# Sparse attention issued head by head, with the depthwise taps of the first channels divided between TensorE and VectorE

## The chip, the cores and the metric

One core of a Trainium2 chip runs the whole program. The metric is the device time of one execution in microseconds. Five engines take part: PE (TensorE matmuls, with its weight loads as a row of their own, PEld), DVE (VectorE), ACT (ScalarE), POOL (GpSimd) and SP (SyncE, which only issues DMAs here). Each engine runs its own instruction list in order and waits on semaphores that the others raise.

## The reference, cut to what matters

One decoder layer over 1024 tokens of width 1024, float32. One projection feeds three mixers; their outputs go through an output projection and a layer norm, then through a mixture of experts and a second layer norm. The change touches the mixers' second half, from the end of the search for the top-k bound to the start of the output projection:

```python
# A: sparse attention, 8 heads, blocks of 128 queries (b = 0..7), causal, top 256 keys of an index score
idx_score = jnp.where(causal, einsum('bqhs,bqh->bqs', relu(logits), iw), -inf)
_, sel = lax.top_k(idx_score, topk)
s = einsum('bqhr,bqkr->bqhk', q_b, c_kv[sel]);  p = softmax(s);  o_lat = einsum('bqhk,bqkr->bqhr', p, c_kv[sel])
# B: pooling over 2/4/8/16 positions, a 64x64 map per group, a scale
# C: GLU, depthwise causal convolution of width 31 over 256 channels, layer norm over channels, silu
h = conv(a * sigmoid(gate), conv_w) + conv_b;  y_c = silu(layer_norm(h, ln_g, ln_b))
mix = concat([y_a, y_b, y_c]) @ w_o
```

The kernel doesn't gather keys: it computes all causal scores of a block (128 queries by `WIDTH[b]` = 128(b+1) keys) and adds a bias that is 0 for chosen keys and very negative for the others.

## The kernel before, in words

All names are those of the source; L numbers are its lines.

**Search.** For blocks 7 to 2 the bound that separates the top 256 scores is found by 25 rounds of bisection (`ROUNDS`). In each round DVE counts over blocks 7, 6 and 2 (L1254) and ACT over blocks 5, 4 and 3 (L955), and DVE updates the bounds (L1269 to L1272). Between its counts ACT copies out projection results; from round to round it takes two of the 16 small `key` and `val` matmul units (PE L605 and L609, ACT L913 and L916), which go through four PSUM banks.

**Convolution.** The 256 channels lie in two halves of 128 partitions. The second half's 31 taps are all on POOL: a multiply (L1613) and an add (L1615) of 128x1024 per tap. Of the first half's taps PE does 18 (`TAPS_PE`) as matmuls with diagonal matrices (L660, two 128x512 matmuls a tap) once all units are through; ACT copies the sum out (L969, which raises `conv0`). POOL does the other 13 after its own 31, again with a multiply and an add each (L1646, L1648).

**Attention.** `attention_steps` writes one list of steps, `STEPS`, and each engine walks through it and does its part of each step. A *pair* is two heads (2j, 2j+1) of one block; there are 32 pairs, the first 16 of blocks 0 to 3 (`SHORT_PAIRS`), then four pairs each of blocks 4, 5, 6 and 7. For a pair:

- `qk`: PE computes the scores of one head and then of the other (L687). A head's 64 channels are partitions 0 to 63 or 64 to 127 of `qT` and `keyT`, so the matmuls use 64 rows of the array. DVE adds the bias, negates, and takes the row extremum in one custom instruction (L1329, "the mask" below). ACT takes the exponential with the row sum (L986).
- `pt`: PE transposes the probabilities (L696), two key blocks of both heads into one PSUM bank of a ring; ACT copies the bank into `pT` (L994).
- `pv`: PE multiplies with the values (L711), and after a pair's last group ACT copies 128x128 into `mix` (L998).
- `choose`: DVE turns the bound of a block into its bias row, in seven instructions (L1286 to L1298). They are strewn among the scores, four a pair at first, then one a pair, then two.
- `rl_set`, `rl`: at a block's end DVE makes the reciprocals of the row sums (L1339, L1340), PE transposes them (L719), DVE multiplies them in (L1345).

The ring has three banks. The scores of the next pair are issued one or two pairs ahead, two heads back to back. After block 6 come `cm` (PE L737, the channel mean, which waits for all taps), `csq`, `cv` (the variance, 128x512 matmuls, ACT takes the root L1011), then `cr` (four DVE reciprocals of 128x256, L1354) and `cn` (DVE multiplies L1359, ACT silu L1015).

**Output projection.** When all steps are done ACT and DVE split `mix` and `w_o` into high and low parts (L1027, L1366, L1369), eight rows of `MIX_ORDER`, and PE multiplies them (L415 to L417).

## Time and profile before

| | |
|---|---|
| median of 3 runs | 1118.24 us (1117.61 to 1118.54) |
| the profiled execution's own time | 1117.91 us |
| its span | 1116.1 us |
| PE busy | 944.8 us (85%) |
| DVE busy | 690.5 us (62%) |
| ACT busy | 564.8 us (51%) |
| POOL busy | 398.5 us (36%) |

The span runs from the first to the last instruction in the trace; the rest of the execution's own time lies around it. Times of events below are counted from the span's start. The stretch that the change touches lies between 194 and 474 us; the output projection, the routing and the experts follow it and are as they were.

### The profile page before, as it was taken

The numbers are of one execution on the slowest core, as the hardware profiler recorded it, in microseconds if no ns is written. First come the engines' busy times: TensorE is split into PE (matmuls) and PEld (weight loads), VectorE is DVE, ScalarE is ACT, GpSimd is POOL, SyncE is SP. The second block draws the span as 40 slices with busy tenths as digits, with TensorE's granted clock in tenths as the row PEclk, the third lists the DMA queues.
The fourth block names the chain that finished last, engine by engine and source line by source line (L and its number), as shares of the span: only waits on it lengthen the run. The fifth ranks groups of instructions, "written<-read, shape, count | busy, mean of one in ns | idle before, by whom it ended". The sixth has DMA issues, their size and how long they took to land.

```text
span 1116.1 us, 15675 instructions
## 1 busy us (share of the span) xinstructions
PE 944.8 (85%) x4724; PEld 729.0 (65%) x4725; DVE 690.5 (62%) x990; ACT 564.8 (51%) x796; POOL 398.5 (36%) x241
## 2 busy tenths in 40 slices
PE   6999999687876778699992599999999999999920
PEld 5877888133443444488882478888887888888820
DVE  4259888985656664463757366688888854334316
ACT  4266576963644446650121265678777744324323
POOL 0000299999999980000000111222323221211116
PEclk8999999888978989999995599999999999999975
DMA  8441120000000000162433747999999988554254
GB/s 230 116 114 38 27 87 1 0 1 0 1 1 1 1 1 1 39 189 85 189 141 121 294 168 233 339 386 397 395 394 399 392 293 264 175 132 106 44 150 189
DMA packets 60972, 171.14 MB, mean 153 GB/s; under 512 B 17120, under 2 KB 31456, under 8 KB 48608
## 3 DMA queue, kind: packets, MB, share of 16 engines
q1 hardware_dynamic: 53584, 143.85, 34.7%
q0 software_dynamic: 7056, 25.69, 9.5%
q10 hardware_dynamic: 288, 1.05, 0.3%
q8 instruction: 24, 0.39, 0.1%
q14 instruction: 20, 0.16, 0.0%
HBM read 141.73 MB, written 26.21 MB: 150 GB/s over the span
## 4 chain that ended last, share of the span: by engine, by line
PE 44%; DMA 12%; DVE 7%; issue 4%; ACT 4%; POOLq 0%; POOL 0%; ACTq 0%; DVEq 0%; SPq 0%
PE ps L415 11%; PE ps L417 10%; PE ps L416 10%; DMA raw<-in_w_gate 10%; PE ps L687 3%; PE ps L696 2%; PE ps L711 2%; ACT probs L986 2%; DVE wlo L1521 2%; PE ps L814 1%; PE ps L763 1%; ACT whi L1070 1%; DVE sm L1389 1%; DMA xg<-x_d,idx_now 1%; PE ps L757 1%
## 5 line engine op out<-in xcount | busy, mean ns | idle before, releaser
L1521 DVE TENSOR_TENSOR wlo<-raw,whi 128x2048 fp32r<-128x2048 f32 x96 | 216.0, 2287 | 52.3 <-ACT whi L1070 51.4
L1070 ACT CAST whi<-raw 128x2048 fp32r<-128x2048 f32 x96 | 180.5, 1911 | 72.6 <-DMA raw<-in_w_gate 41.9
L415 PE MATMUL ps<-whi,xgT_hi 128*128 128x512 f32 x384 | 153.0, 398 | 6.9 <-DVE xgT_lo L1531 6.9
L417 PE MATMUL ps<-whi,xgT_lo 128*128 128x512 f32 x384 | 150.8, 393 | 0.0
L416 PE MATMUL ps<-wlo,xgT_hi 128*128 128x512 f32 x384 | 150.5, 392 | 0.0
L1329 DVE CUSTOM_DVE_ANT_0 probs<-ps,bias 128x128 f32<-128x128 f32 (+7 forms) x64 | 46.0, 755 | 83.1 <-PE ps L687 67.4
L415 PE MATMUL ps<-xT_hi,w_hi 128*128 128x512 f32 (+1 forms) x224 | 87.8, 392 | 4.8 <-DVE w_lo L1159 3.1
L1613 POOL TENSOR_SCALAR tapped<-hpad,par 128x1024 f32<-128x1024 f32 x30 | 89.5, 2984 | 2.9
L415 PEld LDWEIGHTS ps<-whi,xgT_hi 128*128 128x128 f32 x384 | 73.0, 190 | 23.0 <-issue 5.8
L1677 POOL COPY idx_now<-slot_token 128x1 int32 (+1 forms) x24 | 7.5, 313 | 223.2 <-PE ps L814 223.2
L416 PE MATMUL ps<-xT_lo,w_hi 128*128 128x512 f32 (+1 forms) x224 | 86.8, 388 | 0.0
L417 PE MATMUL ps<-xT_hi,w_lo 128*128 128x512 f32 (+1 forms) x224 | 86.6, 387 | 0.0
L696 PE MATMUL ps<-ident,probs 128*128 128x128 f32 x288 | 52.8, 306 | 38.9 <-ACT probs L986 28.6
L417 PEld LDWEIGHTS ps<-whi,xgT_lo 128*128 128x128 f32 x384 | 72.7, 189 | 15.5
L416 PEld LDWEIGHTS ps<-wlo,xgT_hi 128*128 128x128 f32 x384 | 72.8, 190 | 14.4
L1692 POOL DMA_INDIRECT acc_d<-ysb,idx_add x24 | 42.3, 1764 | 105.3 <-ACT ysb L1097 105.3
L986 ACT ACTIVATE probs<-probs,sm 128x128 f32<-128x128 f32 (+7 forms) x64 | 49.1, 768 | 60.5 <-DVE sm L1329 60.5
L415 PE MATMUL ps<-whi,hT_hi 128*128 128x512 f32 x192 | 76.9, 401 | 2.7 <-DVE hT_lo L1543 2.7
L1254 DVE TENSOR_SCALAR_CACHE_REDUCE junk_dve<-bias,sm 128x1024 bf16<-128x1024 f32 (+2 forms) x75 | 75.7, 1009 | 1.8
L417 PE MATMUL ps<-whi,hT_lo 128*128 128x512 f32 x192 | 75.1, 391 | 0.0
L416 PE MATMUL ps<-wlo,hT_hi 128*128 128x512 f32 x192 | 74.9, 390 | 0.0
L696 PEld LDWEIGHTS ps<-ident,probs 128*128 128x128 f32 x288 | 33.4, 151 | 62.6 <-issue 60.3
(273 smaller groups left out, 1934.2 us busy)
## 6 DMA issues: line engine op xcount, KB each, us to landing
raw<-in_w_gate SPq DMA_DIRECT2D x32, 1024.0 KB, 12.5
raw<-in_w_up SPq DMA_DIRECT2D x32, 1024.0 KB, 12.4
raw<-in_w_down SPq DMA_DIRECT2D x32, 1024.0 KB, 10.7
w_raw<-in_w_in SPq DMA_DIRECT2D x14, 512.0 KB, 4.0
x_tok<-in_x SPq DMA_DIRECT2D x8, 512.0 KB, 7.5
wo_raw<-in_w_o SPq DMA_DIRECT2D x16, 256.0 KB, 2.7
x_res<-in_x SPq DMA_DIRECT2D x16, 256.0 KB, 3.4
x_d<-xa SPq DMA_DIRECT2D x4, 512.0 KB, 6.5
```

Source lines behind the costliest of these rows:

```text
L415: pe.matmul(out, l_hi, r_hi, start=start, stop=False)
L416: pe.matmul(out, l_hi, r_lo, start=False, stop=False)
L417: return pe.matmul(out, l_lo, r_hi, start=False, stop=stop)
L687: last = pe.matmul(scores_at(u, WIDTH[b])[:, c:c + n], qT[rows, h // 2, b * P:(b + 1) * P], keyT[rows, h // 2, c:c + n], start=True, stop= ...
L696: last = pe.transpose(out[:, c:c + P], probs_at(score_no(b, 2 * j + h))[:, k * P:(k + 1) * P], ident[:])
L986: act.activation(row, row, ACT.Exp, bias=negmax[:, c:c + 1], scale=-1.0, accum_out=rowsum[:, c:c + 1]).then_inc(exped, 1)
L1070: act.copy(whi[:, n, :], raw[:, n, :]).then_inc(gu_hi if n < 4 else dn_hi, 1)
L1254: dve.tensor_scalar(junk_dve[:, 0:WIDTH[b]], bias[:, AT[b]:AT[b] + WIDTH[b]], now[:, c:c + 1], 0.0, ALU.is_lt, ALU.add, accum_out=res[:, c ...
L1329: dve.tensor_tensor_reduce(out=probs_at(u)[:, 0:WIDTH[b]], in0=scores_at(u, WIDTH[b]), in1=bias[:, AT[b]:AT[b] + WIDTH[b]], scale=-1.0, sc ...
L1521: dve.tensor_tensor(wlo[:, n, :], raw[:, n, :], f32(whi[:, n, :]), ALU.subtract).then_inc(gu_lo if n < 4 else dn_lo, 1)
L1613: pool.tensor_scalar(tapped[:], src, by, None, ALU.mult).then_inc(conv1_mul, 1)
L1692: pool.indirect_dma_start(acc_d, bass.IndirectOffsetOnAxis(ap=idx_add[:], axis=0), ysb[:], None, compute_op=ALU.add).then_inc(y_out, 16)
```

## The change

It rewrites `attention_steps` and what hangs on it:

- The unit is one head (`SCORES`), not a pair. Scores are issued three heads ahead (`AHEAD`), one head at a time. The exponential is a step of its own, two heads ahead. A `pt` group now holds key blocks of one head: all of them for blocks 0 to 3, half of them (`groups`) for blocks 4 to 7. The transposes of a group come ahead of the product of the group before it.
- The ring has two banks instead of three; the freed bank gives the product two banks in turn, so that a pair's product waits for the copy of the pair before the last.
- A `choose` instruction follows every head's scores (two in the first four), not every pair's.
- The 18 taps of PE come earlier: the `key` and `val` units use banks 0, 1, 2 and 7, and from the fifth unit on PE does one tap ahead of each unit, and the last six behind them. The scores of the first three heads are issued before the search has ended.
- The 13 taps of POOL on the first channels go to DVE, fused (multiply and add in one instruction), one behind each of the heads 46 to 58 of 64. POOL does nothing for the first channels.
- `cm` stands three heads before the end, `cv` is 16 matmuls of one column with a root and a reciprocal of 128x8, and two `cb` units spread the result over the channels. The silu moves into the output projection, whose order is now 4, 5, 0, 1, 2, 3, 6, 7.

```diff
-MIX_ORDER = [4, 5, 6, 7, 0, 1, 2, 3]
+MIX_ORDER = [4, 5, 0, 1, 2, 3, 6, 7]
...
+TAPS_DVE = range(46, 46 + TAPS - TAPS_PE)
+TAPS_EARLY = 18
...
+def groups(b):
+
+    cut = (b + 2) // 2 if b >= 4 else b + 1
+    return [range(0, cut)] + ([range(cut, b + 1)] if b >= 4 else [])
+
+
+SCORES = [(b, h) for b, j in PAIRS for h in (2 * j, 2 * j + 1)]
+AHEAD = 3
...
+    for u in range(AHEAD):
+        scores(u)
+    for u in range(2):
+        steps.append(("exp", *SCORES[u]))
+    steps.append(("conv0",))
...
+    for u, (b, h) in enumerate(SCORES):
+        if u + AHEAD < len(SCORES):
+            scores(u + AHEAD)
+        for n in range(len(groups(b))):
+            by_dve = False
+            unit("pt", b, h, n, act=not by_dve, dve=by_dve)
+            if n == 0 and u + 2 < len(SCORES):
+                steps.append(("exp", *SCORES[u + 2]))
+            if waiting:
+                product()
+            waiting.append((b, h, n))
+        while ended:
+            unit("rl", ended.pop(0), act=False, dve=True)
...
+        if u in TAPS_DVE:
+            steps.append(("tap", u - TAPS_DVE[0]))
...
+        def unit_bank(k):
+            return ps[:, 4 + k % 4 if k < PROJECTIONS else (0, 1, 2, 7)[k % 4], :]
...
+            taps = 0
+            for k, between in PLAN[1:]:
+                if k >= PROJECTIONS + 4:
+                    tap(taps)
+                    taps += 1
+                unit(k, between)
+            for w in range(taps, TAPS_EARLY):
+                tap(w)
...
-                    out = ps[:, 4 + r % 3, :]
+                    out = ps[:, 4 + r % 2, :]
...
+                elif kind == "tap":
+                    _, n = step
+                    w = TAPS_PE + n
+                    if n == 0:
+                        dve.wait_ge(conv0, 1)
+                    else:
+                        dve.wait_ge(conv0_rest, n)
+                    dve.scalar_tensor_tensor(conv[:, 0, :], hpad[:, 0, w:w + S], convw[:, w:w + 1], conv[:, 0, :],
+                                             ALU.mult, ALU.add).then_inc(conv0_rest, 1)
...
-            for n, w in enumerate(range(TAPS_PE, TAPS)):
-                pool.tensor_scalar(tapped[:], hpad[:, 0, w:w + S], convw[:, w:w + 1], None, ALU.mult).then_inc(conv0_mul, 1)
-                pool.wait_ge(conv0_mul, n + 1)
-                pool.tensor_tensor(conv[:, 0, :], conv[:, 0, :], tapped[:], ALU.add).then_inc(conv0_rest, 1)
-                pool.wait_ge(conv0_rest, n + 1)
```

How the change moves instructions shows best in three places. A row is one instruction, or `x3` like ones, with what it waits for. First PE in the middle of block 7, before: the scores of two heads stand together, then come groups of four transposes and four products.

```order
L687 MATMUL ps<-keyT,qT 128x512 [waits masked_max]
L687 MATMUL ps<-keyT,qT 128x512
L687 MATMUL ps<-keyT,qT 128x512 [waits masked_max]
L687 MATMUL ps<-keyT,qT 128x512
L696 MATMUL ps<-ident,probs 128x128 [waits exped,ring_dve,ring_act]
L696 MATMUL ps<-ident,probs 128x128 x3
L711 MATMUL ps<-pT,value 64x128 [waits ring_act,mixed]
L711 MATMUL ps<-pT,value 64x128 x3
L696 MATMUL ps<-ident,probs 128x128 [waits exped,ring_dve,ring_act]
L696 MATMUL ps<-ident,probs 128x128 x3
```

The same engine in the same block in the changed kernel (scores L700, transposes L710, products L723):

```order
L700 MATMUL ps<-keyT,qT 128x512 [waits masked_max]
L700 MATMUL ps<-keyT,qT 128x512
L710 MATMUL ps<-ident,probs 128x128 [waits exped,ring_dve,ring_act]
L710 MATMUL ps<-ident,probs 128x128 x3
L723 MATMUL ps<-pT,value 64x128 [waits ring_act]
L723 MATMUL ps<-pT,value 64x128 x3
L710 MATMUL ps<-ident,probs 128x128 [waits exped,ring_dve,ring_act]
L710 MATMUL ps<-ident,probs 128x128 x3
L723 MATMUL ps<-pT,value 64x128 [waits ring_act]
L723 MATMUL ps<-pT,value 64x128 x3
L700 MATMUL ps<-keyT,qT 128x512 [waits masked_max]
```

The scores of a head now stand alone between products and transposes, twice as many times. The second place is PE during the search, where before the units come in one run and the taps behind them:

```order
L605 MATMUL ps<-cT,wuk 128x512 [waits wuk_in,unit_dve,unit_act]
L605 MATMUL ps<-cT,wuk 128x512 [waits unit_dve,unit_act] x7
L609 MATMUL ps<-wuv,cT 128x512 [waits wuv_in,unit_dve,unit_act] x8
L660 MATMUL ps<-hpad,diag 128x512 [waits pads_set,idx_relu,diag_set,unit_dve,unit_act]
L660 MATMUL ps<-hpad,diag 128x512
```

and in the changed kernel (units L610 and L614, taps L661):

```order
L610 MATMUL ps<-cT,wuk 128x512 [waits wuk_in,idx_relu,unit_dve,unit_act]
L610 MATMUL ps<-cT,wuk 128x512 [waits unit_dve,unit_act] x3
L661 MATMUL ps<-hpad,diag 128x512 [waits pads_set,diag_set,unit_dve,unit_act]
L661 MATMUL ps<-hpad,diag 128x512
L610 MATMUL ps<-cT,wuk 128x512 [waits unit_dve,unit_act]
L661 MATMUL ps<-hpad,diag 128x512 [waits diag_set]
L661 MATMUL ps<-hpad,diag 128x512
```

Two tap matmuls now stand ahead of each of the last twelve units. The third place is DVE among the heads of blocks 0 to 3. Before, one `choose` instruction (L1292, L1294) follows two masks (L1329, each with a short row that reads its accumulator):

```order
L1292 SCALAR_TENSOR_TENSOR tie_no<-tied 128x384
L1329 ISA probs,sm<-ps,bias 128x128 [waits ring_mm,qk_mm,dve_chain]
L1329 ISA sm 128x1
L1329 ISA probs,sm<-ps,bias 128x128 [waits ring_mm,qk_mm]
L1329 ISA sm 128x1
L1294 SCALAR_TENSOR_TENSOR tied<-tie_no,sm,tied 128x384
```

and in the changed kernel one follows each mask (L1352):

```order
L1352 ISA probs,sm<-ps,bias 128x128 [waits qk_mm,dve_chain]
L1352 ISA sm 128x1
L1317 SCALAR_TENSOR_TENSOR tied<-tie_no,sm,tied 128x384
L1352 ISA probs,sm<-ps,bias 128x512 [waits ring_mm,qk_mm,dve_chain]
L1352 ISA sm 128x1
L1319 SCALAR_TENSOR_TENSOR tied<-tied,above 128x384
L1352 ISA probs,sm<-ps,bias 128x512 [waits ring_mm,qk_mm,dve_chain]
```

Of the 42 `choose` instructions, 22 stood in the first half of the heads (blocks 0 to 3); now 36 do.

## Rows read from the trace of the kernel before

**Rows 1.** Windows: stretch, length; busy (count) of PE, PEld, DVE, ACT, POOL; TensorE clock

```profile
269.00:326.00 57.00, 43.74 (x305) 24.57 (x303) 37.13 (x91) 32.49 (x99) 55.18 (x21) 0.89 0.00 1
326.00:389.00 63.00, 44.66 (x320) 27.58 (x320) 38.92 (x51) 27.19 (x61) 60.92 (x23) 0.86 0.00 1
425.00:469.00 44.00, 36.48 (x270) 21.68 (x268) 22.38 (x31) 29.15 (x49) 0.00 (x0) 0.97 0.08 25
```

**Rows 2.** Waits from 260 to 471 us: total us, times, longest

```profile
DVE probs L1329 <- PE ps L687: 67.4, 15, 13.4
ACT probs L986 <- DVE sm L1329: 60.5, 29, 3.1
```

**Rows 3.** Timeline: units and taps on PE, end of the search, first mask

```profile
194.62 3.59 PE L605 MATMUL ps<-cT,wuk 128*128 128x512 f32 x8
...
226.22 1.05 ACT L916 COPY value<-ps 128x512 f32<-128x512 f32 x2
...
247.10 0.17 DVE L1277 TENSOR_TENSOR sm<-sm 128x6 f32<-128x6 f32 x1
...
249.69 10.47 PE L660 MATMUL ps<-hpad,diag 128*128 128x512 f32 x24
...
260.71 0.29 DVE L1329 CUSTOM_DVE_ANT_0 probs<-ps,bias 128x128 f32<-128x128 f32 x1 [13.45 <-PE ps L687]
```

**Rows 4.** Timeline: block 3's scores of two heads; first transposes of block 4

```profile
283.56 1.13 PE L687 MATMUL ps<-keyT,qT 64*128 64x512 f32 x4
284.61 0.44 PE L696 MATMUL ps<-ident,probs 128*128 128x128 f32 x2
...
326.72 1.09 PE L696 MATMUL ps<-ident,probs 128*128 128x128 f32 x4 [2.78 <-ACT probs L986]
```

**Rows 5.** Chain of work in block 7, in order of time: start, length

```profile
443.29 0.63 PE ps L696 x4
443.92 0.59 PE ps L711 x8
...
445.68 1.93 PE ps L687 x8
...
451.43 0.63 PE ps L696 x4
```

**Rows 6.** Groups of one line on DVE, 247 to 471 us: busy, mean ns, idle before

```profile
L1329 DVE CUSTOM_DVE_ANT_0 probs<-ps,bias 128x128 f32<-128x128 f32 (+7 forms) x64 | 46.0, 755 | 83.1 <-PE ps L687 67.4 <-issue 15.4
L1292 DVE TENSOR_TENSOR_SCAN tie_no<-tied 128x512 f32<-128x512 f32 (+5 forms) x6 | 12.9, 2154 | 0.1
L1296 DVE SCALAR_TENSOR_TENSOR tied<-tied,above 128x512 f32<-128x512 f32 (+5 forms) x6 | 12.3, 2044 | 0.1
L1298 DVE TENSOR_SCALAR bias<-tied 128x512 f32<-128x512 f32 (+5 forms) x6 | 10.5, 1749 | 0.1
L1290 DVE SCALAR_TENSOR_TENSOR tied<-bias,sm,above 128x512 f32<-128x512 f32 (+5 forms) x6 | 9.1, 1525 | 0.1
L1294 DVE SCALAR_TENSOR_TENSOR tied<-tie_no,sm,tied 128x512 f32<-128x512 f32 (+5 forms) x6 | 9.0, 1504 | 0.1
...
L1286 DVE TENSOR_SCALAR_CACHE_REDUCE above<-bias,sm 128x512 f32<-128x512 f32 (+5 forms) x6 | 5.7, 943 | 0.1
L1345 DVE TENSOR_TENSOR mix<-mix,ps 128x512 f32<-128x512 f32 x8 | 5.5, 686 | 11.3 <-PE ps L719 11.1
```

**Rows 7.** Groups by shape, all engines, 260 to 471 us: busy, mean ns, idle before

```profile
L994 ACT COPY pT<-ps 128x512 f32<-128x512 f32 x64 | 36.4, 578 | 28.3 <-PE ps L696 28.2
...
L986 ACT ACTIVATE probs<-probs,sm 128x1024 f32<-128x1024 f32 x8 | 9.2, 1148 | 10.1 <-DVE sm L1329 10.1
...
L1290 DVE SCALAR_TENSOR_TENSOR tied<-bias,sm,above 128x1024 f32<-128x1024 f32 x1 | 1.3, 1285 | 0.0
```

**Rows 8.** Chain of work at the end of attention: start, length

```profile
469.41 0.70 PE ps L719 x4
...
474.24 0.77 PE ps L415
```

More of the change, by code:

```diff
@@ L87, in score_no, with last_score @@
     return 2 * PAIR_NO[b, h // 2] + h % 2
[L90 to L92 removed]
+def groups(b):
[3 more added lines that the diff above has]
+AHEAD = 3
+def last_score(b):
+    return max(u for u, x in enumerate(SCORES) if x[0] == b)
 def attention_steps():
[L100 removed]
     steps, ring, r_of = [], [], {}
@@ L108, in unit, with scores, product @@
         ring.append((act, dve))
-    def rowsums(p):
-        b = pairs[p][0]
-        if p >= 0 and p == last_no(b):
-            steps.append(("rl_set", b))
-    def scores(p):
-        b, j = pairs[p]
+    def scores(u):
+        b, h = SCORES[u]
         while choices and any(x[1] == b for x in choices):
             steps.append(choices.pop(0))
-        for h in range(2):
-            steps.append(("qk", b, 2 * j + h))
-        rowsums(p - 1)
-        for _ in range(min(4 if p < 2 else 1 if p < SHORT_PAIRS else 2, len(choices))):
+        steps.append(("qk", b, h))
+        for _ in range(min(2 if u < 4 else 1, len(choices))):
             steps.append(choices.pop(0))
-    def after_block(b):
-        unit("rl", b, act=False, dve=True)
-    scores(0)
-    scores(1)
+    def product():
+        b, h, n = waiting.pop(0)
+        steps.append(("pv", b, h, n))
+        if score_no(b, h) == last_score(b) and n == len(groups(b)) - 1:
+            ended.append(b)
+    for u in range(AHEAD):
[3 more added lines that the diff above has]
+    steps.append(("conv0",))
     for i in range(2):
@@ L134, in attention_steps @@
             unit("pw", i, c, act=True, dve=False)
-    ahead = 2
-    waiting = []
-    def product():
-        b, j, n = waiting.pop(0)
-        steps.append(("pv", b, j, n))
-        return b if n == b // 2 and j == HEADS // 2 - 1 else None
-    for p, (b, j) in enumerate(pairs):
-        ended = None
-        for n in range(b // 2 + 1):
-            unit("pt", b, j, n, act=True, dve=False)
-            if len(waiting) == 2:
-                got = product()
-                ended = got if got is not None else ended
-            waiting.append((b, j, n))
-            if n == min(1, b // 2):
-                until = p + 2 if p + 2 < SHORT_PAIRS else p + 1
-                while ahead <= min(until, len(pairs) - 1):
-                    scores(ahead)
-                    ahead += 1
-                if ended is not None:
-                    after_block(ended)
-                    ended = None
-        if ended is not None:
-            after_block(ended)
-        if (b, j) == (NT - 2, HEADS // 2 - 1):
-            assert not choices
+    for u, (b, h) in enumerate(SCORES):
[11 more added lines that the diff above has]
+            unit("rl", ended.pop(0), act=False, dve=True)
+        for e in range(NT):
+            if u + 1 == last_score(e):
+                steps.append(("rl_set", e))
+        if u in TAPS_DVE:
+            steps.append(("tap", u - TAPS_DVE[0]))
+        at = len(SCORES) - 1 - u
+        if at == 3:
             for c in range(2):
@@ L647, in _, with tap @@
             pe.wait_ge(dve_set, 1)
-            for k, between in PLAN[1:]:
-                unit(k, between)
-            pe.wait_ge(unit_act, sum(BY_ACT))
-            pe.wait_ge(unit_dve, sum(BY_DVE))
-            pe.wait_ge(idx_relu, len(IDX))
-            pe.wait_ge(pads_set, 1)
-            for w in range(TAPS_PE):
+            def tap(w):
+                if w == 0:
+                    pe.wait_ge(unit_act, seen(BY_ACT, PROJECTIONS - 1))
+                    pe.wait_ge(unit_dve, sum(BY_DVE))
+                    pe.wait_ge(pads_set, 1)
                 pe.wait_ge(diag_set, w // TAPS_PER_ROUND + 1)
@@ L1024, in _ @@
                 if n < KT:
-                    if n == 0:
-                        act.wait_ge(ring_mm, len(RING_ACT))
+                    if k == 0:
+                        act.wait_ge(mixed, 4 * NT)
+                        act.wait_ge(ring_dve, sum(RING_DVE))
+                    if k == 6:
+                        act.wait_ge(conv_n, 3)
+                        for i in range(2):
+                            act.activation(mix[:, 6 + i, :], conv[:, i, :], ACT.Silu, bias=cvb[:, i:i + 1],
+                                           scale=cvg[:, i:i + 1]).then_inc(conv_y, 1)
+                        act.wait_ge(conv_y, 2)
                     act.copy(mix_hi[:, k, :], mix[:, k, :]).then_inc(mix_hi_s, 1)
```

184 lines of the change are left out of this document (98 added, 86 removed).

## The prediction, made before the changed kernel was run

> **What bounds the kernel now.** I read the windows first. Through the whole attention no engine is full: in the first half of the heads (269 to 326 us) PE is busy 43.7 of 57 us, DVE 37.1, ACT 32.5, and in block 7 PE is busy 36.5 of 44 us [rows 1]. So the stretch is bounded by a loop of waits. The table of waits names it: DVE's masks wait 67.4 us for scores, ACT's exponentials 60.5 us for masks [rows 2]. The chain in block 7 shows the loop: from the transposes at 443.29 to those of the next pair at 451.43 are 8.14 us, 4.07 a head, of which PE's own work is four times (0.59 + 0.59) and 1.93, together 6.65 [rows 5]. The other 1.5 us are mask and exponential of the next pair, for which everything stands still. Ahead of the attention stands a second gap: the search ends at 247.3, but the first mask starts at 260.71, after 13.45 us without work, because PE does its taps until 260 [rows 3]. What follows 474.24 [rows 8] is as it was, so I move it as one piece.
>
> **1. The start.** A tap is two matmuls; 24 rows are 12 matmuls in about 10.3 us, so a tap costs 1.71 us, and eight rows are four units in 3.59 us, 0.90 a unit [rows 3]. The 12 units with a tap ahead cost 2.6 us each. From 198.1 (four units done) PE reaches the last at 229.3; ACT wanted that pair at 226.2 [rows 3]. ACT's counts, and with them the search, come about 2 us late: search done at 249, with hi and lo. The last six taps (10.3 us) end at 240, in the cover of the search, and the scores of heads 0 to 2 behind them. First mask 249 instead of 260.7: 11.7 us won here. Without that cover the six taps would cost their 10.3 us.
>
> **2. First half of the heads (blocks 0 to 3).** Here DVE takes over. The `choose` instructions are 59.5 us for 42 [rows 6], 1.42 us each; 36 stand here now, 51 us, where 22 stood. The 32 masks are 0.29 at 128 columns [rows 3] and 0.755 in the mean of 576 [rows 6], so 0.49 in the mean of these widths (320), 15.7, less 2 where their tails overlap: 13.7 us, `rl_set` and `rl` of four blocks 5.7 us (0.69 for the multiply, the same again for reciprocal and copy), the gaps between linked instructions 2 us, and at each `rl` DVE waits for PE's transposes, some 1 us, 4 in all. Sum 76 us: the mask of head 32, the first of block 4, starts at 325, its transposes at 328. Before they started at 326.7 [rows 4]. So I expect **the whole 11.7 us of the start to be given back by head 32**, and that 14 `choose` instructions are done earlier in return. PE has some 50 us of work here and ACT 40, both below 76.
>
> The price of these instructions rests on POOL, whose taps run under them. The 128x512 form of L1296 and its like vary: L1290 took 1.285 us at 1024 columns [rows 7] and 1.525 us in the mean over narrower ones [rows 6]. The Trainium skill (SBUF — State Buffer, on the shared port pair) says that a VectorE instruction with two SBUF inputs and a GpSimd instruction that reads SBUF exclude each other for a whole instruction. The trace agrees, since 1.525 in the mean exceeds 1.285 for the widest. POOL's second-half taps are not touched, so the bounds are: the same 1.42 us each (taken), or, if every one ran as fast as its columns allow, about 0.8 us each (1.285 scaled to the mean of 704 columns), 22 us less, at which point PE's 50 us bind and head 32 comes some 17 us earlier.
>
> **3. Second half (blocks 4 to 7).** By now everything is three heads ahead and PE should run without waiting. Its work a head: transposes and products cost 0.59 a group of four [rows 5], two transposes 0.44 with a tail under the next [rows 4]; I take 0.15 + 0.11 a key block. Scores: before, two heads stand back to back, and block 3's two 512-column matmuls took 1.05 us together (283.56 to 284.61, [rows 4]), while one 512-column matmul of a tap takes 0.86 [rows 3]. One after the other they would need 1.71, so they ran side by side, each on its 64 rows. In block 7 the pair took 1.93 for four such matmuls instead of 3.4 [rows 5]. **Head by head this is lost**: products stand before and transposes behind, on all rows. I price a head's scores at 0.86 per 512 columns plus 0.15: 1.22, 1.43, 1.65, 1.86 us for blocks 4 to 7; the other bound is half the pair, 0.97 in block 7. I take the dear one, since the row it is nearest to is a lone matmul.
>
> The Trainium skill (TensorEngine Tiling (Array Packing), Key Properties) says that different tiles run in parallel and that a change of tiling mode drains the engine. The rows agree with the first; the second speaks against this change, which doubles the changes into the 64-row mode. The page has no price for a drain; my 0.15 a group holds what the rows show of it, and without it the sum would be 5 us less.
>
> A head then costs PE 2.92, 3.35, 3.79 and 4.22 us (block 4: groups of 3 and 2, block 7: 4 and 4). In block 7 that is more than the 4.07 of before: the pipeline wins the 1.5 us of waiting a pair and loses 1.8 on the scores. ACT has two copies of 0.58, an exponential of 1.15 and half a `mix` copy a head [rows 7], 2.6 us, and fits; its copy of a first group is back 0.1 us after PE's next two groups began, so two ring banks are enough. DVE has a mask (1.2) and a tap (1.285 by the nearest row, two SBUF inputs and 1024 columns [rows 7]), POOL being done by then: 2.5 us, and fits. So 13 fused taps, 17 us, are hidden under PE; if a tap cost over 3 us they would show.
>
> From 328: transposes and products of 32 heads 65.0, scores of heads 36 to 63 44.4, three `rl` 1.9, `cm` 3.9, `cv` 1.5, and 2.5 for ACT's squares and root in the way of the copies: 119.2. Attention ends at 447.3, where before it was 469.4 [rows 8]. `mix` is complete later behind it, since the two `cb` units and four DVE multiplies (2.6 us) stand ahead of the last `rl`: I take 6.0 us to the first projection matmul instead of 4.8. It starts at 453.3 instead of 474.2. Silu is hidden: rows 6 and 7 come last of the eight, over 30 us later.
>
> **Sum.** Start −11.7; first half +13 (choices and waits on DVE, +1.3 net at head 32); second half −23.4 (119.2 for 142.6); tail +1.2. Together −20.9. The profiled execution took 1117.91 us (span 1116.1), 0.3 under the median, so against the median 1118.2 − 20.9 = 1097.3; I say 1098.
>
> **Rivals.**
> - **Scores cheap alone** (half the pair): then 44.4 becomes 24 and ACT and DVE, at 2.6 and 2.5 us a head, come near: −16, about 1081. For it: the 1.93 in block 7 are close to one head's bound. Against: the 1.05 for two block-3 heads.
> - **First half slower still.** The clock of PE was 0.89 there [rows 1] and falls when PE idles, as it will between 240 and 249. At half of the full 2.4 GHz block 3's pair takes double. Eight to ten us of that: 1107.
> - **The first half faster**, because `choose` meets POOL less: down to 17 us less, but PE then binds at a low clock; 8 less is likely, 1090.
> - **Slower than before.** The ring of two banks makes each group serial: transposes wait for the copy of two groups before, products for their own copy, and the copy stands behind an exponential on ACT. A head of block 7 would then be 0.59 + 0.59 + 0.58 + 1.15 + 0.58 + 1.86 plus four hand-overs between engines of about 0.15 each (an estimate: the chain's transposes of four take 0.63 behind a wait and 0.59 without, so it is no less than 0.04): 5.95 us, 1.7 over the forecast, in all 32 heads some 50 us: 1148. It decides from 0.65 us a head on (20.9 over 32). Against it: in the order of steps a whole product group lies between a copy and its reader.
> - **No change**: the scores' loss and the low clock just eat the gain, 1116 to 1120.
>
> **Chances.** Forecast 0.47 (its own range 1092 to 1104), cheap scores 0.15, slower first half 0.18, faster first half 0.12, serial ring 0.05, no change 0.03. From these: faster by over 0.2% (about what a measurement of this kernel can tell from no change) 0.92, within 0.2% 0.03, slower 0.05. The range 1080 to 1109 leaves out the serial ring, no change and the edges.
>
> **What would show it.** Taps on PE end near 240 and the first mask starts near 249; the first transposes of block 4 start near 328 with DVE nearly full before them; a lone head's scores in block 7 take 1.7 to 1.9 us and heads follow at 4.2; the taps on DVE take 1.3 us each and nobody waits for them; the projection starts near 453. I am wrong if scores take 1 us a head, if DVE shows gaps in the first half, or if ACT's copies end the waits of PE.

## The result, and the profile after

The changed kernel is slower: 1150.05 us median (its runs lie between 1143.86 and 1182.36) against 1118.39 for the kernel before on the same chip, a ratio of 1.024, 95% interval 1.013 to 1.035 (ratios leave disturbed runs out, so they need not be the quotient of the medians). The prediction was 1098, faster with a chance of 0.92. The profiled execution took 1143.86 us (span 1141.8), 26 us more than that of before (1117.91).

Four events, read from the two traces, cut the attention into parts. The 16th and the 32nd copy of a product into `mix` (ACT) end the first half of the heads and the whole.

| us from the span's start | before | after | difference | predicted |
|---|---|---|---|---|
| first mask | 260.71 | 247.74 | −13.0 | −11.7 |
| first transposes of head 32 | 326.72 | 346.17 | +19.5 | +1.3 |
| last product ends | 469.4 | 494.3 | +24.9 | −22.1 |
| first matmul of the output projection | 474.24 | 500.56 | +26.3 | −20.9 |

So the start came as forecast. The first half, from the first mask to head 32, took 98.4 us instead of 66.0, and the second 148.1 instead of 142.7, where 119.3 was forecast.

The windows of the changed kernel, in the stretches of [rows 1] (columns as there: busy time and count of PE, PEld, DVE, ACT, POOL, then TensorE's clock):

```profile
269.00:326.00 57.00, 53.43 (x215) 30.06 (x213) 45.44 (x77) 23.73 (x74) 55.28 (x20) 0.75 0.00 1
326.00:389.00 63.00, 63.00 (x276) 38.63 (x275) 24.31 (x45) 24.10 (x64) 11.93 (x5) 0.79 0.00 1
425.00:469.00 44.00, 44.00 (x240) 27.11 (x238) 21.63 (x29) 19.63 (x40) 0.00 (x0) 1.00 0.00 1
```

PE, which was busy 44.66 of 63 and 36.48 of 44 us before, has no free moment left in the second half. Its counts of matmul records (a float32 matmul leaves two, a transpose one) went down all the same, 276 for 320 and 240 for 270: a full PE gets less done. The waits of the changed kernel, 260 to 471 us (total, times, longest):

```profile
ACT pT L1017 <- PE ps L710: 115.6, 57, 4.1
DVE probs L1352 <- PE ps L700: 67.6, 30, 3.9
```

DVE's masks wait for scores as long as before (67.4 us, [rows 2]), but the exponentials' wait for masks, 60.5 us in [rows 2], is gone from the head of the list. In its place ACT's copies wait for PE's transposes. The look-ahead broke the loop of waits as it should, and what is left waits mostly for PE.

Two things made PE full. The first is seen in the chain of block 7, in order of time (start, length), which answers to [rows 5]:

```profile
453.66 1.91 PE ps L700 x4
455.57 0.59 PE ps L710 x4
456.16 1.02 PE ps L723 x8
457.18 0.59 PE ps L710 x4
457.76 1.02 PE ps L723 x8
458.78 1.91 PE ps L700 x4
```

(Each score matmul and each product has two records, so `L700 x4` are a head's two matmuls and `L723 x8` is a group of four products.) A lone head's scores take 1.91 us, as forecast (1.86). Transposes take 0.59 a group as before. But **a group of four products takes 1.02 us, where before it took 0.59** [rows 5]. A head is 5.12 us, 10.24 a pair, where the kernel before took 8.14 with its waits and the prediction said 4.22 a head.

The second is the clock. Windows of two us around 296, and one of the stretch after it:

```profile
294.00:296.00 2.00, 1.45 (x8) 0.70 (x6) 1.97 (x4) 0.90 (x3) 1.92 (x2) 1.00 0.00 0
296.00:298.00 2.00, 0.00 (x0) 0.00 (x0) 2.00 (x1) 0.17 (x2) 1.90 (x2) 0.86 0.00 0
298.00:300.00 2.00, 0.98 (x4) 0.68 (x5) 1.97 (x5) 0.07 (x1) 2.00 (x1) 0.50 0.00 0
...
300.00:348.00 48.00, 48.00 (x135) 26.94 (x135) 26.89 (x47) 14.96 (x44) 37.12 (x14) 0.50 0.00 0
```

PE stood from 295.4 to 299.0, the granted clock fell from 1.00 to 0.50 (from 2.4 to 1.2 GHz), and it stayed there until 352, with PE's records back to back. In these 48 us PE's count is 135 records; in the kernel before it is 213 in the same stretch, with its waits. Why PE stood shows in the timeline, PE first, DVE and POOL behind it:

```profile
294.75 0.70 PE L700 MATMUL ps<-keyT,qT 64*128 64x256 f32 x2
299.02 0.87 PE L710 MATMUL ps<-ident,probs 128*128 128x128 f32 x3 [3.57 <-issue]
...
290.02 2.22 DVE L1369 COPY rlrep<-sm 128x512 f32<-128x512 f32 x1
292.64 2.19 DVE L1315 TENSOR_TENSOR_SCAN tie_no<-tied 128x768 f32<-128x768 f32 x1
295.35 2.85 DVE L1317 SCALAR_TENSOR_TENSOR tied<-tie_no,sm,tied 128x768 f32<-128x768 f32 x1
298.23 0.69 DVE L1374 TENSOR_TENSOR mix<-mix,ps 128x512 f32<-128x512 f32 x1
...
295.04 2.35 POOL L1653 TENSOR_TENSOR conv<-conv,tapped 128x1024 f32<-128x1024 f32 x1
```

The transposes at 299.02 use the ring bank that last held the row sums of block 3. DVE reads that bank in L1374, which stands behind a bias instruction of 2.85 us. DVE was 88 to 99% busy in every 8 us from 244 to 300. The bias instruction is long for its width: the same line took 1.34 us for 896 columns and 1.28 for 1024 later in this trace, and 1.69 for these 768 in the kernel before. It started 0.3 us behind the start of a GpSimd addition and ended 0.8 us behind its end (297.39). So GpSimd's taps of the second half have a share in the stand, as far as one trace can say; no run here takes them away. The stand is put down to "issue" since the profile names no single releaser for it.

An earlier stand is longer. When its taps are done, PE has nothing but the scores of the first heads until ACT has copied the taps' sum out:

```profile
250.81 6.50 PE L738 MATMUL ps<-sums,wpool 128*128 128x512 f32 x8 [11.74 <-ACT conv L1002]
```

The granted clock was 0.50 from 243 to 256, so this costs some 2.8 of the 5.7 us that PE worked until then. Every run below with the early taps has such a stretch, also those under 1100 us.

### The profile page after: what moved, and what is told of

Same layout as the page of the kernel before. It is cut to its first block, busy times and chain, and to the rows that moved or that the text cites. A ratio compares the mean times of both kernels' runs of the same rounds, so it can differ in the third digit from the quotient of the medians.

```text
span 1141.8 us, 15792 instructions
## 1 busy us (share of the span) xinstructions
PE 1022.5 (90%) x4764; PEld 781.9 (68%) x4765; DVE 699.0 (61%) x1002; ACT 564.3 (49%) x810; POOL 326.2 (29%) x215
## 4 chain that ended last, share of the span: by engine, by line
PE 76%; DMA 10%; DVE 9%; ACT 3%; issue 2%; POOLq 0%; POOL 0%; ACTq 0%; SPq 0%; DVEq 0%
PE ps L415 15%; PE ps L417 15%; PE ps L416 15%; PE ps L723 8%; DMA raw<-in_w_gate 7%; PE ps L700 7%; PE ps L710 4%; PE ps L661 2%; PE ps L837 1%; DVE wlo L1559 1%; PE ps L782 1%; ACT whi L1093 1%; DVE junk_dve L1277 1%; DVE bias L1238 1%; DVE sm L1427 1%
## 5 line engine op out<-in xcount | busy, mean ns | idle before, releaser
L1017 ACT COPY pT<-ps 128x512 f32<-128x512 f32 (+3 forms) x96 | 45.9, 478 | 122.4 <-PE ps L710 122.3
L1352 DVE CUSTOM_DVE_ANT_0 probs<-ps,bias 128x128 f32<-128x128 f32 (+7 forms) x64 | 48.5, 757 | 84.0 <-PE ps L700 67.6
L723 PE MATMUL ps<-pT,value 128*64 128x128 f32 x576 | 92.5, 302 | 1.0 <-ACT pT L1017 1.0
L1651 POOL TENSOR_SCALAR tapped<-hpad,par 128x1024 f32<-128x1024 f32 x30 | 92.0, 3067 | 2.9
L700 PE MATMUL ps<-keyT,qT 64*128 64x512 f32 (+3 forms) x192 | 88.4, 575 | 0.0
L723 PEld LDWEIGHTS ps<-pT,value 128*64 128x64 f32 x576 | 67.2, 148 | 19.1 <-issue 16.4
```

What stands on the lines that cost most here:

```text
L700: last = pe.matmul(scores_at(u, WIDTH[b])[:, c:c + n], qT[rows, h // 2, b * P:(b + 1) * P], keyT[rows, h // 2, c:c + n], start=True, stop= ...
L723: last = pe.matmul(product_at(pair_no)[h % 2 * HD:(h % 2 + 1) * HD, :], value[:, k, h * HD:(h + 1) * HD], pT[:, PT_NO[b, h, n] % 3, c * P: ...
L1017: act.copy(pT[:, no % 3, 0:w], src[:, 0:w]).then_inc(ring_act, 1)
L1352: dve.tensor_tensor_reduce(out=probs_at(u)[:, 0:WIDTH[b]], in0=scores_at(u, WIDTH[b]), in1=bias[:, AT[b]:AT[b] + WIDTH[b]], scale=-1.0, sc ...
L1651: pool.tensor_scalar(tapped[:], src, by, None, ALU.mult).then_inc(conv1_mul, 1)
```

## The experiments

Three theories stood at the start. **A**: matmuls on one half of the array no longer run beside their neighbours, products above all. **B** (the serial ring of the prediction's slower rival): PE is held by its hand-overs with ACT. **C**: the low clock from 298 to 352 is the cost.

**products_alternate.** Only the half that a product writes is changed, and with it which product starts and ends a sum.

```diff
-    last = pe.matmul(product_at(pair_no)[h % 2 * HD:(h % 2 + 1) * HD, :],
+    last = pe.matmul(product_at(pair_no)[(h + k) % 2 * HD:((h + k) % 2 + 1) * HD, :],
...
-                     pT[:, PT_NO[b, h, n] % 3, c * P:(c + 1) * P], start=k == 0, stop=k == b)
+                     pT[:, PT_NO[b, h, n] % 3, c * P:(c + 1) * P], start=k <= 1, stop=k >= b - 1)
```

> The changed kernel, with one thing altered: the products of consecutive key blocks of a head go to the two 64-channel halves of the output in turn, instead of all to the head's own half. So it leaves the sums of a head split over both halves (its attention output is not the reference's); number and size of all instructions stay. Theory A (side by side: a product fills 64 columns of the array, and two neighbours on different column halves overlap, as the pair's did before; in the changed kernel all four of a group stand on one half and come one after the other): a group of four in block 7 falls from 1.02 us to 0.59, block 7's head from 5.13 to about 4.3, and the whole from 1144 to 1105 to 1122. Theory B (PE is held by its hand-overs with ACT: two ring banks, wait on every copy): the same 1144 within 3 us, product groups stay near 1.0. Theory C (the low clock from 298 to 346 us is the cause, the products cost what they cost): second half unchanged, so 1140 to 1147.

Its runs spread from 1129 to 1173 us, ratio 1.014 to before (1.008 to 1.020), so its time misses A's range and settles little. Its trace does, once the clock is full again (PE in block 7):

```profile
487.45 1.98 PE L700 MATMUL ps<-keyT,qT 64*128 64x512 f32 x4
489.37 0.66 PE L710 MATMUL ps<-ident,probs 128*128 128x128 f32 x4
489.95 0.66 PE L723 MATMUL ps<-pT,value 128*64 128x128 f32 x8
490.54 0.66 PE L710 MATMUL ps<-ident,probs 128*128 128x128 f32 x4
491.13 0.66 PE L723 MATMUL ps<-pT,value 128*64 128x128 f32 x8
491.72 1.98 PE L700 MATMUL ps<-keyT,qT 64*128 64x512 f32 x4
```

From start to start a group of products is 0.59 again (489.95 to 490.54), and the head 4.27 us (487.45 to 491.72), 0.05 from my 4.22. Same instructions, same waits, another half: A holds for the products, B falls. The saving was lost elsewhere in the traced execution, which took 1170.67 us: its clock was at 0.50 in both of these stretches, from about 287 to 454 us:

```profile
300.00:348.00 48.00, 48.00 (x152) 24.32 (x153) 32.01 (x51) 15.48 (x48) 41.11 (x15) 0.50 0.00 0
348.00:396.00 48.00, 48.00 (x162) 24.96 (x160) 10.97 (x22) 14.04 (x37) 0.00 (x0) 0.50 0.00 1
```

A rival is left for the 0.59: in the changed kernel the four products of a group also add to one sum in PSUM, and might wait for each other there. The rows speak against it. Groups of two, three and four products take 0.58, 0.80 and 1.02 us in the changed kernel, so 0.22 for each further one, and 128 of the 512 columns of a tap matmul (0.86 us) are worth 0.215: the lone products run at a tap matmul's pace without waiting, and half of that, 0.11, is what two at a time give. That is argued; no run here separates the two.

**scores_alternate.** From block 4 on the second 512 columns use the other 64 rows.

```diff
+    hr = (h + c // 512) % 2
+    rows = slice(hr * HD, (hr + 1) * HD)
     last = pe.matmul(scores_at(u, WIDTH[b])[:, c:c + n], qT[rows, h // 2, b * P:(b + 1) * P],
                      keyT[rows, h // 2, c:c + n], start=True, stop=True)
```

> The changed kernel, with one thing altered: from block 4 on the second 512 columns of a head's scores are computed on the other 64 rows of the array (from the other head's channels, so these scores are not the reference's); number and size of instructions stay. Theory A (side by side): a lone head of block 7 falls from 1.91 us to about 1.0 to 1.1, the 32 heads of blocks 4 to 7 save 16 to 24 us in all (block 4 only little, its second piece has 128 columns), 1144 becomes 1120 to 1130. Theory B (hand-overs): shorter scores turn into waiting, 1140 to 1144. Theory C (low clock): no more than 5 us.

1148.2 us, which looks like nothing won. But the wrong scores also change the routing behind the attention. The records of one kind of the experts' matmuls number 400 here and 384 in the changed kernel, 16 a tile, so one expert tile more is computed; from the start of the projection to the end of the span are 661.6 us instead of 641.2, and 20.4 us less would be 1127.8, inside A's range. The attention itself is shorter: the projection starts at 485.43, 15.1 us earlier than in the changed kernel. Between the 16th and the 32nd copy into `mix` lie 128.5 us instead of 145.8, 17 less. A head's scores in block 7 take 1.06 us (454.67 to 455.73) instead of 1.91. A holds here too, with the size expected (16 to 24).

**both_alternate** has both edits.

> Both alterations of the two runs before together (attention output not the reference's). Theory A: the gains add up until ACT or DVE bind (ACT has 2.6 us a head in block 7, DVE 2.5 with a tap, PE then 3.4): 1085 to 1102, faster than the kernel before (1118), so that order head by head would have paid had its matmuls still overlapped. Theory B: 1135 or more. Theory C: 1130 or more.

1105.8 us, ratio 0.989 (0.985 to 0.992), a little above the range. The projection starts at 460.43, 40 us earlier than in the changed kernel. In block 7 a head takes 3.41 us (425.88 to 429.29). It had the low clock too, from 284 to 345, behind a stand of 1.32 us at 282. So order head by head would pay only if its matmuls overlapped, and even then less than expected, for the clock.

**choose_spread.** Back to one bias instruction behind every second head of the short blocks.

```diff
-    for _ in range(min(2 if u < 4 else 1, len(choices))):
+    for _ in range(min(2 if u < 4 else u % 2 if u < 2 * SHORT_PAIRS else 1, len(choices))):
```

> The changed kernel, with the instructions that make bias rows set back to one behind every second head of the short blocks, as before the change; the rest of them follow one a head in the long blocks. PE stood 3.57 us at 299 in the changed kernel, behind DVE, and its granted clock was 0.50 from there to 346 (where block 4's heads cost 4.73 us). Theory C (that gap brings the low clock): the gap goes, the clock stays at 1.00 through 299 to 346, and 12 to 22 us come back: 1122 to 1132. Theory A (PE is full for want of overlap, the clock falls by itself or for other gaps): the time moves by less than 5 us, 1139 to 1147.

1121.2 us, ratio 1.003 (1.001 to 1.006): some 25 us come back in the profiled execution (1118.44 for 1143.86), a little more than C's 12 to 22. (The 4.73 us in the expectation counts a head's scores and first group only; the whole head is 6.83, 343.74 to 350.57, for 3.72 at full clock here, 321.64 to 325.36.) The windows:

```profile
300.00:348.00 48.00, 47.30 (x251) 28.86 (x249) 32.02 (x56) 23.50 (x70) 37.75 (x14) 1.00 0.00 1
348.00:396.00 48.00, 48.00 (x256) 29.57 (x255) 29.87 (x44) 21.17 (x51) 0.00 (x0) 1.00 0.01 1
```

251 records at 1.00 where the changed kernel had 135 at 0.50. The longest stand of PE between 255 and 350 was 0.70 us. Head 32 comes at 322.91, 23 us earlier. The second half is as it was (144.5 us between the two copies, for 145.8), with products of 1.02 and heads of 5.12. This run moves the bias rows and so DVE's load and the clock together. The next one moves PE's stand alone.

**gap_filled.**

```diff
     last.then_inc(ring_mm, 1)
+    if b == 3:
+        pe.wait_ge(mixed, 8)
+        for n in range(24):
+            pe.transpose(ps[:, 7, P:2 * P], ident[:], ident[:])
```

> The changed kernel with 24 idle transposes (about 3.5 us of PE work at full clock, into unused columns of a product bank) behind the row-sum transposes of block 3, the place at which PE stood 3.57 us at 299 in the profiled run and after which the clock was 0.50 until 346. Nothing else moves, DVE's work neither. Theory C (it is PE's standing there that brings the low clock): the gap is filled, the granted clock stays at 1.00, 1144 becomes 1119 to 1126, as where the bias rows were spread. Rival (the clock falls whatever PE does there, or the bias rows cost the time through DVE): 1143 to 1150.

1137.1 us, ratio 1.015 (1.009 to 1.021), between the two. The stand at 299 is gone and the clock is 1.00 there, DVE being nearly as full as before (87 to 98% in every 8 us from 244 to 300). A stand of 1.12 us at 280.5 had left the clock at 1.00. But the next row sums, block 1's, make the next stand, for the copy L1373 (2.21 us at 316.11) behind a bias instruction:

```profile
318.47 0.63 PE L731 MATMUL ps<-ident,rlrep 128*128 128x128 f32 x4 [1.37 <-DVE rlrep L1373]
```

```profile
316.00:318.00 2.00, 1.09 (x8) 0.68 (x7) 1.97 (x2) 0.48 (x1) 2.00 (x1) 1.00 0.00 0
318.00:320.00 2.00, 1.53 (x6) 0.90 (x7) 1.97 (x5) 0.86 (x3) 1.90 (x2) 0.94 0.00 0
320.00:322.00 2.00, 2.00 (x8) 1.23 (x7) 1.97 (x5) 0.29 (x1) 1.92 (x2) 0.50 0.00 0
```

The low clock now begins at 320 and ends about 340, and the first half ends 11 us earlier (337.4 for 348.6). The fall moved with the stand, which speaks against the rival. C is shown for the place; its full price did not come back.

**ring_of_three.** The ring at three banks again, the products at one.

```diff
-    out = ps[:, 4 + r % 2, :]
+    out = ps[:, 4 + r % 3, :]
...
-    return ps[:, 6 + pair_no % 2, 0:P]
+    return ps[:, 7, 0:P]
```

The waits are set to match.

> The changed kernel with the ring set back to three banks and the products to one. The gap at 299 stood before a transpose group whose bank had last held block 3's row sums, which DVE read only at 298.23, behind a bias instruction of 2.85 us. Theory D (the second bank of the products, taken from the ring, makes that gap): with three banks PE has another group before it must wait for DVE, the gap is gone or under 2 us, and in most runs the clock stays: 1119 to 1130. Theory C without D (DVE would be late in any ring): 1140 to 1150. Cost of the single product bank: a wait for ACT's copy, 0 to 0.3 us a pair, up to 9 us.

Inconclusive in time: 1143.3 us median, ratio 1.011 (1.004 to 1.018), with three of six runs near 1130 to 1135 and three near 1151 to 1154, none of them in D's range. The profiled one (1135.38) has clock 1.00 from 260 to 468, no stand over 0.7 us between 285 and 360, and ends its first half at 327.5, 21 us before the changed kernel. So that execution fits D: with the third bank back the stand is gone, though its bias instruction of 768 columns still took 2.45 us. The one product bank costs in the second half (154.3 us for 145.8): 8.0 us of waits for ACT's copies into `mix`, 15 of them, at the upper end of what was expected. What the runs near 1150 met, no trace shows.

**both_alternate_spread.** Both alterations of the array halves, and the bias rows spread.

> Both earlier alterations together, bias rows spread and matmuls side by side (attention output not the reference's). If the two causes are independent and the only ones: projection starts near 475.4 - 30 = 441 to 448, 1084 to 1092 in all, provided the number of expert tiles is that of the reference. If they are one cause (shorter PE work leaves gaps that bring the low clock anyway): 1098 or more.

1090.6 us, ratio 0.974 (0.968 to 0.979), and the projection starts at 442.58, inside the 441 to 448. Against choose_spread (475.44) the side-by-side matmuls are worth 32.9 us. Against the changed kernel the projection starts 25.1 us earlier in choose_spread, 40.1 in both_alternate and 58.0 here, so the two causes add up but for 7 us. The low clock came once more, behind a stand of 2.48 us that ended at 322.38, for 17 us.

**The parts that the change could have had alone.** start_alone is the kernel before with the taps of PE during the search and nothing else.

```diff
+            return ps[:, 4 + k % 4 if k < PROJECTIONS else (0, 1, 2, 7)[k % 4], :]
...
+                if k >= PROJECTIONS + 4:
+                    tap(taps)
+                    taps += 1
                 unit(k, between)
```

> The kernel before, with only the early taps: PE's 18 taps among and behind the units during the search, the units in banks 0, 1, 2 and 7. Pairs, ring of three and POOL's taps as before. If the start's gain is real and lasts (all theories): first mask near 248 instead of 260.7 and 1105 to 1109. If the first half is held by DVE's bias rows, as my prediction had it, the gain is eaten by head 32: its first transposes still near 324 to 327, and 1115 to 1118.

1105.9 us, ratio 0.990 (0.988 to 0.991). First mask at 249.74, end of the first half 318.1 (before 330.6), projection at 461.26 (before 474.24): the start's 11 to 13 us last to the end. They are not given back by head 32 as long as the bias rows keep their old pace.

dve_taps_alone is the kernel before with the 13 taps fused on VectorE.

```diff
+        if p in TAPS_DVE:
+            steps.append(("tap", p - TAPS_DVE[0]))
...
-            for n, w in enumerate(range(TAPS_PE, TAPS)):
-                pool.tensor_scalar(tapped[:], hpad[:, 0, w:w + S], convw[:, w:w + 1], None, ALU.mult).then_inc(conv0_mul, 1)
```

> The kernel before, with only the 13 taps of the first channels moved from GpSimd to VectorE, fused, one behind each of the pairs 15 to 27. If they lie in DVE's idle time, as the trace of the changed kernel says (1.28 us each, nobody waits): 1116 to 1120, or some us less where DVE's other instructions had met GpSimd (down to 1110). If they hold up masks: 13 x 1.3 us, 1130 to 1135.

1116.4 us, ratio 0.998 (0.995 to 1.001): hidden.

pairs_ahead keeps the pairs of before and takes over only the look-ahead.

```diff
     for p, (b, j) in enumerate(pairs):
...
+        until = p + 2 if p + 2 < SHORT_PAIRS else p + 1
+        while ahead <= min(until, len(pairs) - 1):
+            scores(ahead)
+            ahead += 1
...
         for n in range(b // 2 + 1):
             unit("pt", b, j, n, act=True, dve=False)
...
+            if n == 0:
+                steps.append(("exp", bb, 2 * jj))
+            if n == min(2, b // 2):
+                steps.append(("exp", bb, 2 * jj + 1))
```

> The kernel before, with only the look-ahead: pairs as before (scores, transposes and products of two heads together), but the next pair's scores stand ahead of this pair's first transposes, and the exponentials are steps of their own, behind this pair's first and third copy. Theory A (overlap lost is the fault, look-ahead as such is good): block 7's pair falls from 8.14 us to 6.7 to 7.2, second half 12 to 20 us less: 1096 to 1108. Rival (the loop of waits doesn't break, since mask and exponential only move their wait to ACT's copies): 1114 to 1120.

1104.6 us, ratio 0.989 (0.987 to 0.990). A pair of block 7 takes 7.06 us (434.55 to 441.61) instead of 8.14. At its block 6 GpSimd's last tap ends at 416.43 and `cm` begins at 416.67, and PE waits 1.5 us for it: the taps on GpSimd have just come into the path. The longest stands that are left, 7.49 us ending at 359.98, 7.30 ending at 391.13 and 4.96 ending at 331.03, are all before the row-sum transposes, which now wait for DVE's copy `rlrep`.

pairs_ahead_all adds to it the early taps, the fused taps (in the pairs 20 to 29), the cheap variance, the silu inside the output projection and its new order.

> Pairs with look-ahead as in the run before, and all that was independent of going head by head: early taps, 13 fused taps on VectorE, the variance as columns with its spreading units. Theory A: the start's 12 us and the 12 to 20 us of the look-ahead add up: 1085 to 1098, faster than both. If the first half is DVE's: the start's gain is eaten there, 1096 to 1106.

**1083.0 us, ratio 0.969 (0.966 to 0.972), 35 us faster than the kernel before**, 2 us under the expected range. The projection starts at 436.19. The chain in block 7, whose gaps (left out) are work of ACT and DVE on the way to the next product:

```profile
406.26 0.66 PE ps L738 x8
406.92 0.59 PE ps L723 x4
407.51 0.59 PE ps L738 x8
408.10 1.93 PE ps L714 x8
...
412.46 0.56 ACT pT L1032
413.02 0.18 ACT mix L1036
413.20 0.04 issue
413.24 0.32 PE ps L738
```

Two heads' scores in 1.93, four products in 0.59, and 6.98 us a pair. PE's own 6.65 are nearly all of it. What it still loses is again before the row-sum transposes: stands of 6.87, 3.05 and 4.00 us behind DVE (ending at 318.50, 343.09 and 369.77).

pairs_ahead_early_bias is that kernel with two bias instructions a short pair instead of one.

```diff
-    for _ in range(min(4 if p < 2 else 1 if p < SHORT_PAIRS else 2, len(choices))):
+    for _ in range(min(4 if p < 2 else 2, len(choices))):
```

> The pairs with look-ahead and all the rest (1083 us), with two bias instructions a pair among the short blocks instead of one, so that 36 of 42 stand there, as in the changed kernel. If the rate of the bias rows among the short blocks is what holds DVE and then PE (my prediction's step 2), here too: first half 10 to 20 us longer, 1092 to 1105. If it mattered only together with head-by-head order: 1080 to 1086.

1098.3 us, ratio 0.981 (0.976 to 0.986), 15 us slower than with the old pace. Its first half ends at 336.9 instead of 313.1, 24 us later where 10 to 20 were expected. The windows of this kernel, and then of pairs_ahead_all:

```profile
252.00:300.00 48.00, 34.74 (x170) 18.03 (x171) 43.68 (x70) 20.90 (x62) 46.55 (x17) 0.71 0.00 1
300.00:324.00 24.00, 16.07 (x114) 9.23 (x112) 23.66 (x34) 11.95 (x37) 23.27 (x9) 0.86 0.00 1
```

```profile
252.00:300.00 48.00, 39.88 (x264) 20.91 (x263) 39.52 (x91) 30.50 (x92) 46.45 (x18) 0.94 0.00 1
300.00:324.00 24.00, 16.33 (x108) 10.40 (x110) 14.94 (x20) 8.70 (x24) 23.27 (x9) 0.79 0.00 1
```

DVE is nearly full (43.68 of 48, 23.66 of 24) and PE has 170 records for 264. So the early bias rows cost in pairs too, without going head by head. What share of that is PE waiting and what share its lower clock (0.71 for 0.94) these windows do not tell apart.

## Why the prediction was wrong, step by step

The projection of the changed kernel starts at 500.56 where 453.3 was forecast. Of these 47.3 us, 18.2 are there at head 32 (346.17 for 328) and 28.9 come in the second half.

**1. The start: right.** −11.7 predicted, −13.0 measured, and the taps end at 238.4 (predicted 240):

```profile
227.95 10.47 PE L661 MATMUL ps<-hpad,diag 128*128 128x512 f32 x24
...
247.74 0.29 DVE L1352 CUSTOM_DVE_ANT_0 probs<-ps,bias 128x128 f32<-128x128 f32 x1
```

**2. The first half: the kind right, its consequence mis-sized.** I had DVE full with 36 bias instructions until head 32, at 328. DVE was nearly full, until 300, and pairs_ahead_early_bias shows that the early bias rows cost in the other order too. But what decided was what the late bias instruction did to PE: PE stood, and the clock fell. The forecast's sum had no term for the clock in this half. I had it as a rival, "first half slower still", with 8 to 10 us and a chance of 0.18, for another place (240 to 249). At that place it came too (clock 0.50 from 243 to 256, some 2.8 us). At 299 the stand and the low clock behind it, together with the bias rows that caused them, cost 23 us at head 32 (346.17 for 322.91 in choose_spread). That the low clock would last 50 us while PE had work all the time was in no row I read; in [rows 1] its mean is 0.89 and 0.86. PE's work in this half, "some 50 us", was also too small: in choose_spread, at full clock and without a wait over 0.7 us, it takes from 259.4 to 322.9, 63.5 us. The error of step 3 is in it once more: 80 key blocks at 0.107 make 8.6 of the 13.5 us. The 4.9 that are left were not taken apart. In choose_spread it is PE that is full there, not DVE (38.8 of 63.5). The bias instructions of the changed kernel were a little cheaper than forecast, 55.5 us for 42 or 1.32 each for 1.42; that is as far as the rival of a faster first half came true. (Its bound "about 0.8 us each" should have been 0.88, 1.285 scaled from 1024 columns to 704, and 19 us less instead of 22.)

**3. The second half: this is the step that failed most.** I wrote "transposes and products cost 0.59 a group of four", and priced a product group of the new order like that, at 0.15 us and 0.11 a key block. The products there cost 0.22 a key block. The row was right and its reading wrong. In the order of before the four products of a group belong to two heads in turn (the loop over `h` stands inside that over `k`); one head writes partitions 0 to 63 of the output, the other 64 to 127. They ran side by side, just as the scores did, and products_alternate brought the 0.59 back. I had seen that for the scores and taken it out of their price, and had not asked the same of the `L711` group with its `64x128` outputs. The sum of the second half, by its own terms: 208 key blocks are 52 groups of four, at 0.43 more each, 22.4 us. The half clock up to 352 adds 2.9 (5.9 us for the work of 2.9). At the end `cv` takes 3.72 instead of 1.5, and behind it the clock is at 0.50 once more (488 to 492) and the last groups take some 2 us more. Together 29.5 for the 28.9 that are missing (148.1 for the sum of 119.2); the smaller terms, dearer scores (0.05 in 28 heads) and ACT's copies (1.0 of the 2.5 set aside), cancel. The price of the scores was right: 1.27 in block 4 (1.22), 1.91 in block 7 (1.86).

The Trainium skill (TensorEngine Tiling (Array Packing), When to Use Tiling) names both cases: row tiling where the contraction is 64 or less, and column tiling where the left-hand (stationary) side has 64 columns or less. The products are of the second kind (`128*64` in their rows), and the trace agrees: 0.59 on two halves in turn, 1.02 on one. I had drawn on the same page for the scores alone.

**Tail: right.** 6.2 us behind the last product for 6.0. **Fused taps: right**, 13 at 1.280 us, nobody waits for them.

**The rivals.** The serial ring, my case for slower, gave 1148 and so nearly the measured time, but by luck, through a mechanism that the trace refutes: PE waits 1.0 us for ACT's copies in all of 260 to 495, and products_alternate runs 4.27 us a head through the same ring. "Scores cheap alone" is refuted by 1.91 us.

What remains open: which stands bring the low clock, and what ends it. Under records that stand back to back it lasted 17 to 21 us (both_alternate_spread, gap_filled), 51 to 62 (the changed kernel, scores_alternate, both_alternate) and 167 in products_alternate's execution of 1170.67 us. The kernel before, whose loop of waits makes PE stand for over 1 us 23 times between 264 and 465 us, had eight such stretches in that time, of 4 to 8 us each, and the five stands of 1.91 to 2.38 us between 352 and 393 brought none, among them

```profile
385.12 0.63 PE L696 MATMUL ps<-ident,probs 128*128 128x128 f32 x4 [2.04 <-ACT probs L986]
...
392.77 0.63 PE L696 MATMUL ps<-ident,probs 128*128 128x128 f32 x4 [2.38 <-ACT probs L986]
```

with the clock at 1.00 from 374 to 400. In pairs_ahead_all the longest stand, 6.87 us, brought about 7 us of it. So a stand came ahead of each long stretch of low clock, but its length does not say how long the stretch will be.

## What to carry to other kernels

When a change reorders matmuls that use half of the array's rows or columns, look at every group in the chain for neighbours on different halves: its measured time is a price of that order, not of the instruction. Take a gap out of a loop by issuing further ahead within the order that overlaps (here pairs), not by splitting the order. And cost an early, longer queue on one engine by where it makes TensorE stand: in the order head by head stands of 1.3 to 3.6 us were followed by 17 us and more at half the clock, where the kernel before lost 4 to 8 us at a time.

## What the runs showed of the hardware

- In six traces (changed kernel, scores_alternate, both_alternate_spread, gap_filled, both_alternate, products_alternate) the granted clock fell to 0.50 during a stand of PE or within some 2 us behind it; the stands were 3.57, 3.62, 2.48, 1.37, 1.32 and 1.31 us. In choose_spread and ring_of_three no stand in that part was over 0.83 us, and the clock stayed at 1.00. It also stayed at 1.00 over a stand of 1.12 us in gap_filled and over five of 1.91 to 2.38 us in the kernel before (352 to 393 us).
- After the fall it stayed at 0.50 for 17 to 62 us in five of the six, and for 167 in products_alternate, though PE's records stood back to back. The Trainium skill (TensorE: Matmul & The Clock Gate, HAM oscillation) describes idle gaps that bring the half clock back. The six traces agree in that each fall came with a stand; that the half clock outlasts the gap many times over under full work, the runs here show beside it.
- A product of 128x64 by 128x128 takes 0.255 us alone on its half and 0.147 with its neighbour on the other (1.02 and 0.59 for four, the group's own 0.15 in it). A 64-row score matmul of 512 columns takes 0.95 alone and 0.48 beside another (1.91 and 1.93 for two and for four).
- GpSimd's 13 multiply-and-add taps took 5.7 us each in the mean in the kernel before (3.24 and 2.50), the fused form on VectorE 1.28.
- A bias instruction on VectorE with two inputs in SBUF (768 columns) took 2.85 us beside a GpSimd addition and ended 0.8 us behind it; the same line took 1.28 for 1024 columns once GpSimd was idle.
